# Two-layer hybrid decoder step: conditioning slices placed after other output tiles, one round of them in the first down projection, and the last columns turned during the last residual

## The reference

```python
mod = (jax.nn.silu(c) @ w_ada + b_ada)[:, None, :]            # w_ada 1024 x 6144: the conditioning
sh1, sc1, g1, sh2, sc2, g2 = jnp.split(mod, 6, axis=-1)
hn = rmsnorm(x, norm1_g) * (1.0 + sc1) + sh1
xl, gl, bs, cs, hs = jnp.split(hn @ w_in, 5, axis=-1)         # w_in 1024 x 2560
xc, new_lc = causal_conv(xl, st_lc, lru_conv_w)
xc = xc + lru_conv_b
r = jax.nn.sigmoid(block_diag(xc, lru_wa, lru_ba))            # the gates
ig = jax.nn.sigmoid(block_diag(xc, lru_wx, lru_bx))
h_seq, h_last = rglru(xc, r, ig, lru_lambda, st_h)            # a scan over the tokens
zc, new_sc = causal_conv(cs * hs, st_sc, sc_conv_w)
mix = jnp.concatenate([h_seq * gelu(gl), bs * zc], -1) @ w_out
x = x + g1 * mix
hn2 = rmsnorm(x, norm2_g) * (1.0 + sc2) + sh2
u, v = jnp.split(hn2 @ ffn_w_up, 2, axis=-1)                  # 1024 x 5632
uc, new_fc = causal_conv(u, st_fc, ffn_conv_w)
x = x + g2 * ((gelu(uc) * v) @ ffn_w_down)                    # 2816 x 1024
```

## Time and profile before

| | |
|---|---|
| runs | 1356.6, 1352.7, 1356.3 us; median 1356.3 |
| profiled execution | 1355.5 us, of which the span is 1353.9 |
| TensorE, share of the span busy | 97% |
| VectorE, ScalarE, GpSimd | 53%, 35%, 4% |
| mean granted clock of TensorE | 0.986 of full |
| data moved | 157 MB, 116 GB/s over the span |

### The profile page before, as it was taken

One profiled execution on the slowest core, in us unless ns is written; L12 is line 12 of the kernel. 1 busy time (PEld: TensorE's weight loads), 2 busy tenths in 40 slices (PEclk: granted clock), 3 DMA queues, 4 the chain that ended last, 5 costly groups with the idle time before them and its releaser, 6 DMA issues.

```text
span 1353.9 us, 23506 instructions
## 1 busy us (share of the span) xinstructions
PE 1315.4 (97%) x9667; PEld 1253.2 (93%) x9667; DVE 713.8 (53%) x1252; ACT 474.4 (35%) x623; POOL 47.6 (4%) x94
## 2 busy tenths in 40 slices
PE   5799999999999999999999999999999999999998
PEld 3688888899999999999999788999999999999997
DVE  2761683585445443445487158468554454344445
ACT  4532562363222321223344157336322232133231
POOL 3000000000000000000020000000000000000001
PEclk7799999999999999999999999999999999999999
DMA  9545555532222122122233645312222222222212
GB/s 330 175 139 173 187 189 204 189 103 78 79 93 93 62 94 93 63 93 86 69 122 99 219 172 185 125 63 94 78 78 94 93 77 78 94 67 88 93 34 94
DMA packets 108669, 157.10 MB, mean 116 GB/s; under 512 B 3543, under 2 KB 100792, under 8 KB 102453
## 3 DMA queue, kind: packets, MB, share of 16 engines
q1 hardware_dynamic: 101269, 112.56, 24.9%
q0 software_dynamic: 7168, 43.47, 9.2%
q10 hardware_dynamic: 160, 0.05, 0.0%
HBM read 153.08 MB, written 2.99 MB: 115 GB/s over the span
## 4 chain that ended last, share of the span: by engine, by line
PE 91%; DVE 4%; DMA 3%; ACT 1%; issue 1%; SPq 0%; POOLq 0%; DVEq 0%
PE ps L346 25%; PE ps L348 24%; PE ps L347 24%; PE ps L365 4%; PE ps L366 4%; PE ps L367 4%; PE ps L418 4%; DMA ada_w<-in_w_ada 2%; PE ps L523 1%; DVE w_lo L871 1%; PE ps L458 1%; DMA work<-in_w_ada 1%; DVE work L947 0%; PE ps L481 0%; ACT w_hi L609 0%
## 5 line engine op out<-in xcount | busy, mean ns | idle before, releaser
L346 PE MATMUL ps<-norm_hi,w_hi 128*128 128x288 f32 x1792 | 533.9, 298 | 0.0
L347 PE MATMUL ps<-norm_lo,w_hi 128*128 128x288 f32 x1792 | 529.2, 295 | 0.0
L348 PE MATMUL ps<-norm_hi,w_lo 128*128 128x288 f32 x1792 | 527.5, 294 | 0.0
L346 PEld LDWEIGHTS ps<-norm_hi,w_hi 128*128 128x128 f32 x1792 | 336.5, 188 | 18.4 <-issue 16.8
L348 PEld LDWEIGHTS ps<-norm_hi,w_lo 128*128 128x128 f32 x1792 | 338.1, 189 | 0.0
L347 PEld LDWEIGHTS ps<-norm_lo,w_hi 128*128 128x128 f32 x1792 | 337.2, 188 | 0.0
L871 DVE TENSOR_TENSOR w_lo<-w_raw,w_hi 128x2048 fp32r<-128x2048 f32 x92 | 210.6, 2289 | 97.2 <-ACT w_hi L609 97.1
L609 ACT ACTIVATE w_hi<-w_raw 128x2048 fp32r<-128x2048 f32 x92 | 175.7, 1910 | 150.0 <-PE ps L348 137.3
L346 PE MATMUL ps<-mid_hi,w_hi 128*128 128x288 f32 x704 | 209.2, 297 | 0.0
L347 PE MATMUL ps<-mid_lo,w_hi 128*128 128x288 f32 x704 | 207.7, 295 | 0.0
L348 PE MATMUL ps<-mid_hi,w_lo 128*128 128x288 f32 x704 | 207.0, 294 | 0.0
(11 more groups left out here) (198 smaller groups left out, 1375.1 us busy)
## 6 DMA issues: line engine op xcount, KB each, us to landing
w_raw<-in_ffn_w_up SPq DMA_DIRECT2D x44, 1024.0 KB, 5.1
ada_w<-in_w_ada POOLq DMA_DIRECT2D x40, 1024.0 KB, 5.2
w_raw<-in_w_in SPq DMA_DIRECT2D x20, 1024.0 KB, 5.3
w_raw<-in_ffn_w_down SPq DMA_DIRECT2D x16, 1024.0 KB, 5.1
w_raw<-in_w_out SPq DMA_DIRECT2D x8, 1024.0 KB, 5.2
w_raw<-in_ffn_w_down SPq DMA_DIRECT2D x8, 768.0 KB, 4.4
work<-in_w_ada SPq DMA_DIRECT2D x4, 1024.0 KB, 11.6
work<-in_x_prompt SPq DMA_DIRECT2D x4, 512.0 KB, 5.3
```

The source lines that it names most:

```text
L346: T.matmul(out, WH[:, r, k, c:c + P], xh[:, k, h, :], start=start, stop=False)
L347: T.matmul(out, WH[:, r, k, c:c + P], xl[:, k, h, :], start=False, stop=False)
L348: last = T.matmul(out, WL[:, r, k, c:c + P], xh[:, k, h, :], start=False, stop=stop)
```

## The change

- **Where the slices stand.** `slice_after(n)` now takes the slice's number. Slices 0 and 1 follow tiles 4 and 5 as before, none follows tile 6, and slices 2 to 15 follow tiles 7 to 20, each one tile later than before, in both layers. The turns move from after tiles 12 and 20 to after tiles 14 and 21. ScalarE's stream keeps its two copies `ada_rows(l * 3 + 2)` and `ada_rows(l * 3 + 3)` where they were.
- **VectorE's modulations.** The second moves from after `lru_scan(1)` to after `sc_product(1)`, the third from after the first residual of the output projection to after the second one and its split.
- **Layer 0's last round** (for layer 1) leaves the output projection and follows the eight tiles of the first down projection. The copy, the turn and the modulation of this round come one group later.
- **The end.** Seven of eight transposes of rows 3 and 4 are done before the statistics of half 1 and the eighth right after; for this row 4 uses banks 4 and 5, and these statistics bank 2.

```diff
@@ stat_bank, Y_BANK
-        def stat_bank(h):
-            return PS[:, B_R + h, 400:406]
+        def stat_bank(m, h):
+            return PS[:, 2 if m == 2 * L + 1 and h else B_R + h, 400:406]
...
-        Y_BANK = [6, 4, 6, 0, 2, 6]
+        Y_BANK = [6, 4, 6, 0, 4, 6]
...
@@ tensor: the slices
-                def slice_after(t):
-
-                    i, k = (t - 4) // 8, (t - 4) % 8
-                    if t == 4:
+                def slice_after(n):
+
+                    if n == 0:
                         pe.wait_ge(psum_free[1], l * PL + 3)
-                    if i < rounds:
-                        if k == 0:
-                            pe.wait_ge(ada_rows_ready, l * 3 + (i + 1))
-                        ada_slice(l * 24 + (8 + 8 * i + k), k)
+                    if n % 8 == 0:
+                        pe.wait_ge(ada_rows_ready, l * 3 + (n // 8 + 1))
+                    ada_slice(l * 24 + 8 + n, n % 8)
...
-                    if t in (12, 20):
-                        if t == 12:
-                            pe.wait_ge(gate_read, l * 8 + 4)
-                        ada_turn(l * 3 + (2 if t == 12 else 3))
-                    slice_after(t)
+                    if t in (14, 21):
+                        if t == 14:
+                            pe.wait_ge(gate_read, l * 8 + 6)
+                        ada_turn(l * 3 + (2 if t == 14 else 3))
+                    if t != 6 and t < 21:
+                        slice_after(t - (4 if t < 6 else 5))
...
-                            if c == 2:
+                            if c == 3:
                                 pe.wait_ge(mod_ready, l * 3 + 2)
...
-                def after_w_out(h, i, k):
-                    between(h, i, k)
-                    if i % 2 == 1 and k == KX - 1:
-                        slice_after(T_WOUT + 4 + 2 * h + i // 2)
-
-                half_tiles_of_last_four(l * PL + T_WOUT // 2 + 2, l * 2 + 2, after_w_out)
+                half_tiles_of_last_four(l * PL + T_WOUT // 2 + 2, l * 2 + 2, between)
...
+                    if g == 1 and l < L - 1:
+                        ada_turn(l * 3 + 4)
                     if g == 0 and l < L - 1:
-                        ada_turn(l * 3 + 4)
+                        for i in range(8):
+                            tile(l * PL + i // 4 * 2 + T_DN[g] // 2, i % 4, MH, ML, range(K),
+                                 (mid_ready, l * 30 + made) if i == 0 else None)
+                            slice_after(16 + i)
+                        made += K
+                        continue
...
@@ tensor: the end
+            pe.wait_ge(psum_free[0], read(L - 1, T_DN[2] + KX - 2))
+            pe.wait_ge(x_ready, L * 24 - 1)
+            y_part(3, range(KX - 1))
+            pe.wait_ge(y_rows, 2)
+            y_part(4, range(KX - 1))
+            norm_stats(L * 2 + 1, 1)
+            for j in (3, 4):
+                y_part(j, [KX - 1]).then_inc(y_cols, 1)
             pe.wait_ge(y_rows, 3)
-            norm_stats(L * 2 + 1, 1)
-            for j in (3, 4, 5):
-                y_tile(j)
+            y_tile(5)
...
@@ scalar: the copy of the round for layer 1
-                def end_of_sqrt():
-                    if l < L - 1:
-                        ada_rows(l * 3 + 4)
...
+                        if g == 0 and l < L - 1:
+                            ada_rows(l * 3 + 4)
...
@@ vector: the modulations
-                modulation(l * 3 + 2, 16, CUR[:, 16:32])
                 split(l, 7)
                 sc_product(0)
                 sc_low(0)
                 sc_product(1)
+                modulation(l * 3 + 2, 16, CUR[:, 16:32])
                 split(l, 8)
...
-                    if m == 0:
+                    if m:
+                        sum_square(l * 2, m - 1)
+                    if m % 2:
+                        split(l, 12 + m // 2)
+                    if m == 1:
                         modulation(l * 3 + 3, 32, CUR[:, 32:48])
...
-                    if g == 0 and l < L - 1:
+                    if g == 1 and l < L - 1:
                         modulation(l * 3 + 4, MOD_SH1, BNEXT[:])
```

More of the change, by code:

```diff
@@ L432, in norm_stats @@
                 for t0, w, c in half_tiles(h):
-                    last = T.matmul(stat_bank(h)[0:w, c:c + 1], acc_of(m, h)[:, t0:t0 + w], AVG[:, 0:1],
+                    last = T.matmul(stat_bank(m, h)[0:w, c:c + 1], acc_of(m, h)[:, t0:t0 + w], AVG[:, 0:1],
                                     start=True, stop=True)
@@ L475, in _, with y_part @@
             ada_turn(1)
+            def y_part(j, ks):
+                i, h, t0, w = token_tiles()[Y_ORDER[j]]
+                for k in ks:
+                    last = T.transpose(PS[0:w, Y_BANK[j] + k // 4, (k % 4) * P:(k % 4 + 1) * P], X[:, k, h, t0:t0 + w], IDN[:])
+                return last
             def y_tile(j):
[L479 to L482, removed]
+                y_part(j, range(KX)).then_inc(y_cols, 1)
             pe.wait_ge(mod_ready, 1)
@@ L542, in _ @@
                 between = norm_in_jobs(l * 2 + 2, (gate_read, l * 8 + 8))
[L544 to L549 removed]
+                half_tiles_of_last_four(l * PL + T_WOUT // 2 + 2, l * 2 + 2, between)
                 pe.wait_ge(mod_ready, l * 3 + 3)
[L551 removed]
+                first_quad(l * PL + T_UP[0] // 2, l * 2 + 2, norm_in_quad(l * 2 + 2), (ada_rows_ready, l * 3 + 3))
                 for i in range(4):
@@ L628, in std @@
                 act.wait_ge(stat_done, m * 2 + (h - 1))
-                A(STD[:, 3 * h:3 * h + 2], stat_bank(h)[:, 3 * h:3 * h + 2], ACT.Sqrt, bias=EPST[:])
-                A(STD[0:HS, 3 * h + 2:3 * h + 3], stat_bank(h)[0:HS, 3 * h + 2:3 * h + 3], ACT.Sqrt,
+                A(STD[:, 3 * h:3 * h + 2], stat_bank(m, h)[:, 3 * h:3 * h + 2], ACT.Sqrt, bias=EPST[:])
+                A(STD[0:HS, 3 * h + 2:3 * h + 3], stat_bank(m, h)[0:HS, 3 * h + 2:3 * h + 3], ACT.Sqrt,
                   bias=EPST[0:HS, :]).then_inc(std_ready, 1)
@@ L658, in norm_round, with end_and_norm @@
                 A(k_pair(NH, p, h), f, ACT.Copy).then_inc(norm_hi, 1)
-            def end_and_norm(l, e, split0, split1, sh, between):
+            def end_and_norm(l, e, split0, split1, sh):
                 m = e + 2
@@ L676, in end_and_norm @@
                 split_halves(*split1, part=1)
-                between()
                 root_mean(m, 1)
@@ L789, in _ @@
                         split(l, 12 + m // 2)
-                def end_of_sqrt():
-                    if l < L - 1:
-                        ada_rows(l * 3 + 4)
-                end_and_norm(l, l * 2, (l, T_UP[0] // 2), (l, T_UP[0] // 2 + 1), MOD_SH2, end_of_sqrt)
+                end_and_norm(l, l * 2, (l, T_UP[0] // 2), (l, T_UP[0] // 2 + 1), MOD_SH2)
                 act.preload_act_table(ACT.Gelu_apprx_tanh)
@@ L837, in _ @@
                         if l < L - 1:
-                            end_and_norm(l, l * 2 + 1, (l, PL), (l + 1, 1), MOD_SH1, lambda: None)
+                            end_and_norm(l, l * 2 + 1, (l, PL), (l + 1, 1), MOD_SH1)
                     made += K
@@ L1216, in _ @@
                         gains(MOD_SC2, V_N2)
[L1217 to L1220, removed]
                 if l < L - 1:
```

1 line of the change is left out of this document (removed).

## The result

The kernel before took 1354.99 us (median of 4 runs, 1352.66 to 1356.59), the changed one 1379.99 us (1378.33 to 1381.07): a ratio of 1.0188 (95% interval 1.0172 to 1.0204), 25.0 us slower. The forecast was 1378; it started from the 1356.3 us of earlier runs, so as a difference 22.0 us were forecast and 25.0 measured. The profiled execution took 1380.5 us with a span of 1378.9, against 1355.5 and 1353.9. The 25.0 us are those of the spans too.

A forecast was written before the change was run, and what follows sets the result against it. TensorE, busy 97% of the span, was taken as the bound, so only its waits and clock count: 15.0 + 5.2 - 5.7 + 1.6 + 7.2 - 1.3 = +22.0 us on 1356.3, giving 1378 us, range 1368 to 1390.

The forecast's parts named there:

- two waits ahead of tile 14: Both layers: ScalarE's copy, held by the later slice, delays VectorE's product, so TensorE waits 7.5 us each, +15.0 us.
- clock after them: After the two waits ahead of tile 14: lower TensorE clock, 2 x 2.6 = +5.2 us, ends 0 and 6.8.
- other waits for `ada_w` in the stages of tiles 4 to 20: Layer 1's two later waits of 0.6 us, at tiles that keep their slices, were left as they are.
- norm in layer 0's output projection: Without the last round's slices, TensorE waits 0.5 us for `x_tmp` and about 1.1 for `norm_lo`: +1.6 us (0 to 2.2).
- waits in the down projection: Layer 0's short down tiles: seven waits of 0.94 us for `ada_w` plus collisions, +7.2 us, ends 5.9 and 12.2.
- clock after the first of them: Layer 0's first down projection: the main forecast counted no lower clock after the waits for `ada_w`.
- a slice between down tiles, against one between half tiles: Layer 0's moved last round: the amount of TensorE's work was taken as unchanged, so 0.
- the end: Last statistics: VectorE's waits of 0.91 and 0.35 us for columns after `rstd` go, -1.3 us (0 to -1.5).
- part 2: No slice after tile 6: waits of 2.06 and 1.89 us for `ada_w` and 1.7 of clock go, -5.7 us.
- Rival (b): Down projection: each of seven waits lowers the clock, 1.7 us each, +11.9 us, 1390 us; chance 0.08.
- The covers: Other work behind the later slices stays hidden: slack 2 us at tile 16 and 1 us at tile 22.

The follow-up runs named there:

- experiments 1 and 2: Changed kernel with ScalarE's copy `ada_rows(l * 3 + 2)` moved behind `split(l, 7)` (first: 1362.52 us) or between `gates(1)` and `root(1)` (second: 1364.38 us).
- experiment 3: Changed kernel with layer 0's last round after the last eight tiles of the first up projection instead of the down tiles: 1372.57 us.
- Experiment 7: Kernel before plus no slice after tile 6, the new end, and the copy behind `split(l, 7)`; layer 0's last round in the output projection: 1350.71 us, ratio 0.9966.
- experiment 6: Kernel before with only the end changed, seven transposes of rows 3 and 4 ahead of the last statistics: 1355.18 us, ratio 0.9986.

## Why the prediction was right, step by step

| term | predicted | measured |
|---|---|---|
| two waits ahead of tile 14 | 2 x 7.5 = 15.0 | 2 x 7.58 = 15.2 |
| clock after them | 5.2 | 1.7 + 2.7 = 4.4 |
| no slice after tile 6 | -5.7 | -5.65 |
| other waits for `ada_w` in the stages of tiles 4 to 20 | 0 | +0.65 |
| norm in layer 0's output projection | 1.6 | 3.1 |
| waits in the down projection | 7.2 | 6.9 |
| clock after the first of them | 0 | 1.5 |
| a slice between down tiles, against one between half tiles | 0 | 0 |
| the end | -1.3 | -1.3 |
| sum | +22.0 | +24.8 of 25.0 |

- **The waits ahead of tile 14** held to 0.1 us, and experiments 1 and 2 show the mechanism. All times in that stretch came some 5 us earlier than those worked out, since the gain of part 2 and one slice fewer lie ahead of it, but ScalarE's, VectorE's and TensorE's moved together: TensorE was ready at 159.54 (164.5 predicted), the product ended at 166.97 (172.0). The idle time before the copy was put at some 14 us, and was 15.98; that was a slip, since the prediction's own times (6.25, and a copy at 154.88 instead of 145.15) give just this.
- **The clock** was sized by its nearest row, the wait of 3.5 at the start. Tile 14 took 8.36 and 9.33 instead of 6.65, so of two waits of the same 7.58 us one cost 1.7 and the other 2.7. The windows show where the difference lies: TensorE ran at the lower level for 3.9 us after the first wait (167.12 to 171) and for 6.1 after the second (833.94 to 840). Why the clock stayed down longer there is open; in experiment 3, where the two waits are 7.57, the tile took 8.39 and 8.57, so 2.7 is the odd one of four.

```profile
167.00:171.00 4.00, 3.88 (x16) 3.92 (x17) 3.17 (x5) 3.97 (x4) 0.00 (x0) 0.50 0.34 118
171.00:176.00 5.00, 5.00 (x42) 4.82 (x44) 0.59 (x3) 4.94 (x8) 0.00 (x0) 1.00 0.01 3
834.00:840.00 6.00, 6.00 (x25) 6.00 (x26) 3.71 (x6) 5.94 (x8) 0.00 (x0) 0.50 0.18 62
840.00:845.00 5.00, 5.00 (x40) 3.99 (x39) 1.26 (x2) 4.08 (x5) 0.00 (x0) 1.00 0.02 3
```

- **Part 2.** The waits of 2.06 and 1.89 and the fall of the clock behind the first are gone, as forecast. The loads behind them were slow ones (7.9 and 7.7 us, issued 1.4 us after a weight load); they still take 8.1 and 7.8, but now have two tiles. The sentence "I leave them" on the two waits of 0.6 was the weak one: the rounds now run one tile later against the weight loads, and there are waits of 0.86 in layer 0 and 1.01 in layer 1 in their place (1.87 against 1.22). The loads behind these took 6.7 and 6.9 us, issued 1.6 us after a weight load; before, the load at this point was issued 2.2 us after it and took 5.4 and 6.4. Experiment 7 shows the same more strongly: a skipped slice gave back nearly nothing of the waiting, only its place and so the clock.
- **The down projection** had nearly its right total, for partly wrong reasons. Of the seven expected waits six are there. Five have 0.71 to 1.06 and a mean of 0.90, where 0.94 was worked out (the terms as written, 0.71 + 5.1 - 4.92, give 0.89). The first is 2.12, because its load was issued at 357.95, 0.57 us after a weight load (357.38), and landed after 6.4 instead of 5.2. That is the collision that the sum counted at 0.15 for each of four and the upper end at 1.4. This first weight load is issued when VectorE's split ends at 357.35, in the very stretch in which the first slice is done. Behind that wait the next tile took 6.56 us instead of 5.05, part of it at the lower clock, and its load so landed in time: the missing seventh wait is hidden under 1.5 us of lost clock. Rival (b) was therefore right once, behind the one wait that was twice as long; the waits of about 1 us left the clock at full. The stage grew by 17.84 us: eight slices at 1.18 (next point), 1.5 of clock, and 6.9 that the waits cost, of which the list shows 6.6.
- **A slice's own place** costs nothing, as the sum had it ("the amount of its work does not change"). Without a wait, the last matmul ahead of a slice and the first one behind it start 1.22 us apart, between half tiles in the kernel before and between down tiles in the changed one alike. As matmuls in a row start 0.13 apart and the first two after a slice 0.1 more, a slice lengthens a stage by 1.18.

```profile
265.23 0.29 PE L367 MATMUL ps<-mid_hi,w_lo 128*128 128x288 f32 x1
...
266.45 0.41 PE L365 MATMUL ps<-mid_hi,w_hi 128*128 128x288 f32 x1
...
355.97 0.29 PE L348 MATMUL ps<-mid_hi,w_lo 128*128 128x288 f32 x1
...
357.19 0.40 PE L346 MATMUL ps<-mid_hi,w_hi 128*128 128x288 f32 x1
```

- **The norm in layer 0's output projection** is the term that was too small by most. The waits of 0.70 and 1.03 us are where they were expected, but the stage lost more than the list of waits shows: the second piece lost eight slices, gained one, and lost a turn (7 x 1.18 + 0.44 = 8.7 us) and is only 5.57 shorter, so the norm costs 3.1, more than the 2.2 that it was given as its upper end. The trace before had shown it. There layer 1's stage, without a round, takes 132.05 us, and layer 0's, less eight slices and a turn, 139.04 - 9.44 - 0.44 = 129.2: 2.9 us between them. The prediction took the two waits of the list in place of this difference. Where the 1.4 us beyond the listed waits lie, one pause by another, was not worked out.
- **The covers** named in the prediction held: no wait at tile 16 or 22. The end gave 1.3 us.

The norm (1.5), the clock in the down projection (1.5) and the new waits of part 2 (0.65) came out over the forecast, the clock ahead of tile 14 (0.8) and the waits in the down projection (0.3) under it. With the small differences that is 2.8 of the 3.0 us between 22.0 and 25.0; the start, 0.34 us shorter by itself, makes it half a microsecond that is not assigned. (The forecast's low end was added up with 1 for the clock ahead of tile 14 and 0.5 for the norm, whose own lower ends were 0; with 0 it would be +13 instead of +15, still inside the range as widened.) So the mechanism and the main term were right, and the sum came close also because its errors partly cancelled.

## What to carry to other kernels

When a producer is moved later, look at every engine that copies its result: an in-order engine stands still at that copy, and everything written behind it, however unrelated, is late with it; moving the copy was worth 18 us here, with the slices left where the change put them. Compare a single-buffered load's time from issue to landing, and the 0.7 us or so until it is issued, with the work between its two uses before choosing tiles for it, and put it behind the longest ones. To price what a stage loses without some of its work, compare two stages with and without it as a whole; a list of waits leaves out the short pauses. A wait that disappears from one place is not yet won: add up the list of waits by releaser, and see whether another place has taken it.

## What the runs showed of the hardware

- **The clock after a wait for a load.** Over these nine traces, TensorE's waits for `ada_w` in the middle of the work were followed by a lower granted clock (0.66 over the next 5 us where a window was read) when they had lasted 2.81, 2.16, 2.12, 2.06 and 2.04 us, and by none when they had lasted 2.00, 1.89, 1.71, 1.61, 1.52 or less. The sizes sort without exception, but 0.04 us between the two groups, in ten waits with other work around each, is no more than an observation. With the 1.5 to 1.7 us of clock behind it, a wait of 2.04 to 2.12 cost 3.6 to 3.8 us in all, and one of 1.89 only itself. The same code in layer 1 fell on either side in two executions (1.89 in the kernel before, 2.16 in experiment 6), so one trace does not tell what such a wait costs. Two windows, of the first experiment behind its wait of 2.04 and of the second behind its wait of 2.00, stand on either side:

```profile
355.00:360.00 5.00, 4.80 (x25) 3.40 (x26) 2.29 (x1) 0.17 (x1) 0.54 (x1) 0.66 0.24 51
...
358.00:363.00 5.00, 5.00 (x39) 4.72 (x36) 1.62 (x1) 0.00 (x0) 0.54 (x1) 1.00 0.55 175
```

- **A load issued shortly after another.** In the changed kernel's down stage, a load of `ada_w` took 6.4 us when a weight load (768 KB, from another engine's queue) had been issued 0.57 us before it. The other six took 5.0 to 5.3, those beside the weight loads of 1 MB issued 0.6 to 1.9 us later (366.75, 382.40, 396.33) among them. Over all nine traces, from 60 us on, the same holds: all 37 full loads issued within 1.6 us after a weight load took 6.3 to 8.7 us, and those issued 2.0 to 2.5 us after one 5.0 to 6.4. Of the other 273, 237 took 4.9 to 5.4, but single ones up to 7.6 (201.54 in experiment 7, the load behind its wait of 1.71) with no weight load issued in the 4 us ahead, so the distance to the last weight load is not the only thing that counts. With half the bytes the loads took 3.8 to 4.4, one 5.0, and 5.5 behind a weight load. No run moved a weight load alone, so that the two share something is read from their distance and not shown.
